# The last expert fold placed inside the preceding down product, and the slot sums turned by halves

## What is computed

```python
combine = jnp.sum(jax.nn.one_hot(global_idx, N_EXPERTS) * weights[..., None], axis=1)
y = jnp.zeros_like(x2d)
for e in range(N_EXPERTS):                       # 32 experts, each token chooses 2
    h = jax.nn.silu(x2d @ w_gate[e]) * (x2d @ w_up[e])
    y = y + combine[:, e:e + 1] * (h @ w_down[e])
```

## Time and profile before

| | |
|---|---|
| median of 3 runs | 1796.92 us |
| profiled execution: its own time | 1800.9 us |
| its span, first to last instruction | 1799.1 us |
| mean granted TensorE clock | 0.993 |
| PE busy | 1763.1 us (98%) |
| PE weight loads | 1528.9 us (85%) |
| DVE busy | 1157.0 us (64%) |
| ACT busy | 927.2 us (52%) |
| weights read | 317.74 MB, 177 GB/s over the span |

### The profile page before, as it was taken

The page is one execution under the profiler, slowest core; times in us unless marked ns, Lnnn a source line. Parts: engine busy times, 40 slices in busy tenths (PEclk is TensorE's granted clock), DMA queues, the critical chain, the costliest instruction groups (busy, mean ns, idle before and its releaser), DMA issues.

```text
span 1799.1 us, 25837 instructions
## 1 busy us (share of the span) xinstructions
PE 1763.1 (98%) x10654; PEld 1528.9 (85%) x10654; DVE 1157.0 (64%) x1452; ACT 927.2 (52%) x1239; POOL 116.7 (6%) x82
## 2 busy tenths in 40 slices
PE   7999999999999999999999999999999999999999
PEld 6999888899998888888898888888888988988887
DVE  5955577677775765468968655455545897765553
ACT  6444364466664644366754544354444666455442
POOL 1423011000000000000210000000000013000000
PEclk9999999999998999999999999999999999999999
DMA  8420135599997355545224555556554632346552
GB/s 275 133 74 1 43 111 213 189 391 387 383 386 274 117 187 187 184 146 185 71 95 141 179 183 184 183 183 187 187 187 152 199 118 71 118 142 208 183 181 106
DMA packets 179862, 320.47 MB, mean 178 GB/s; under 512 B 6560, under 2 KB 149280, under 8 KB 168096
## 3 DMA queue, kind: packets, MB, share of 16 engines
q1 hardware_dynamic: 179600, 318.29, 52.0%
q0 software_dynamic: 144, 0.52, 0.1%
HBM read 317.74 MB, written 1.05 MB: 177 GB/s over the span
## 4 chain that ended last, share of the span: by engine, by line
PE 87%; DVE 8%; ACT 3%; DMA 1%; issue 1%; POOL 0%; SPq 0%; DVEq 0%
PE ps L557 83%; PE ps L560 4%; DVE ring_lo L1592 2%; DVE arena L1581 2%; ACT arena L2454 1%; ACT rhi L2454 1%; DMA ring<-in_w_in 1%; ACT L2454 0%; DVE xnl L1581 0%; DVE small L2240 0%; DVE arena L2392 0%; DVE arena L1584 0%; POOL arena L3052 0%; DVE arena L2342 0%; DVE arena L1791 0%
## 5 line engine op out<-in xcount | busy, mean ns | idle before, releaser
L1592 DVE TENSOR_TENSOR ring_lo<-ring,rhi 128x2048 fp32r<-128x2048 f32 x266 | 608.7, 2290 | 267.0 <-ACT rhi L2454 266.6
L2454 ACT ACTIVATE rhi<-ring 128x2048 fp32r<-128x2048 f32 x266 | 503.7, 1904 | 145.3 <-PE ps L557 125.2
L557 PE MATMUL ps<-rhi,xnh 128*128 128x512 f32 (+2 forms) x784 | 307.9, 393 | 0.0
L557 PE MATMUL ps<-ring_lo,xnh 128*128 128x512 f32 (+2 forms) x800 | 307.4, 384 | 0.0
L557 PE MATMUL ps<-rhi,xnl 128*128 128x512 f32 (+2 forms) x784 | 302.2, 385 | 0.0
L557 PE MATMUL ps<-xnh,rhi 128*128 128x256 f32 (+1 forms) x760 | 221.3, 291 | 4.1 <-DVE xnl L1581 3.2
L2454 ACT ACTIVATE arena<-ps 128x512 f32<-128x512 f32 (+4 forms) x194 | 97.1, 518 | 244.9 <-PE ps L557 165.5
L557 PE MATMUL ps<-xnl,rhi 128*128 128x256 f32 (+1 forms) x760 | 215.9, 284 | 0.0
L557 PE MATMUL ps<-xnh,ring_lo 128*128 128x256 f32 (+1 forms) x760 | 215.8, 284 | 0.0
L557 PE MATMUL ps<-rhi,hhi 128*128 128x512 f32 x544 | 207.1, 397 | 0.0
L557 PE MATMUL ps<-arena 128*128 128x64 f32 (+11 forms) x1446 | 171.0, 291 | 6.1 <-DVE arena L2362 3.7
(11 more groups left out here) (249 smaller groups left out, 2131.5 us busy)
## 6 DMA issues: line engine op xcount, KB each, us to landing
ring<-in_few_gu SPq DMA_DIRECT2D x60, 1024.0 KB, 7.3
ring<-in_w_in SPq DMA_DIRECT2D x45, 1024.0 KB, 5.4
ring<-in_ffn_w_gate SPq DMA_DIRECT2D x88, 512.0 KB, 4.0
ring<-in_ffn_w_up SPq DMA_DIRECT2D x88, 512.0 KB, 5.0
ring<-in_ffn_w_down SPq DMA_DIRECT2D x44, 1024.0 KB, 4.9
ring<-in_exp_w_down SPq DMA_DIRECT2D x32, 1024.0 KB, 7.4
ring<-in_w_out SPq DMA_DIRECT2D x20, 1024.0 KB, 4.9
ring<-in_w_in SPq DMA_DIRECT2D x4, 896.0 KB, 4.7
```

Source lines behind the costliest of these rows:

```text
L557: return e.matmul(o, lhsT, rhs, start=start, stop=stop, skip_group_check=True)
L1592: e.tensor_tensor(lo, raw, f32(hi), SUB).then_inc(*w.hit("lo", n))
L2454: return e.activation(o, x, func, **kw)
```

## The change

Five things change.

1. SBUF layout: comb shrinks from 64 to 8 words, expert_of moves up behind it (56 words), first_slot becomes 48 words and stands last. Every later tile lies 128 bytes lower.
2. PE: for the last block the order becomes product(32, 0), turn(31), product(32, 1), first half of down(31), turn(32), second half of down(31), down(32). down(32) writes its halves to two banks (4 and 5) and signals each.
3. DVE: `few_place(31)` stands behind `few_gated(32)`; `few_place(32)` is two copies of half the size, each with its own wait and signal.
4. ACT: the split of the first `ffn(0)` tile stands behind `few_hidden(32)` instead of ahead of it.
5. `slot_sums`: PE turns the first halves of slots 0, 1 and 2 once the first half of the last copy is there, then the second halves; slot turn 2 uses banks 6 and 7. Spreads follow in another order. Work counts stay the same.

```diff
-        comb_ = sb("comb", 64)
+        comb_ = sb("comb", 8)
+        expert_of = sb("expert_of", 56, I32)
...
-        first_slot = sb("first_slot", NK, I32)
-        expert_of = sb("expert_of", 40, I32)
+        first_slot = sb("first_slot", 48, I32)
...
+        y_bank = [0, 2, 6, 0]
...
-            def few_down(j):
+            def few_down(j, halves=(0, 1)):
...
+                for half in halves:
+                    if BLOCKS[j][2]:
+                        b = 4 + 2 * (j % 2) + (half if j == NK - 1 else 0)
+                        if j == NK - 1:
+                            bank(b, ("few_y", j, half))
+                        elif not half:
+                            bank(b, ("few_y", j, 1))
+                        for dc in range(4 * half, 4 * half + 4):
...
+                    if half or j == NK - 1 or not BLOCKS[j][2]:
                         p.then_inc(*w.hit("few_down", j, half))
...
-                w.wait_ge("few_y", NK - 1, 1)
-                turn(0)
-                turn(1)
-                sum_banks("moe")
+                for half in range(2):
+                    w.wait_ge("few_y", NK - 1, half)
+                    for j in range(3):
+                        turn(j, half)
                 spread(0, 0)
-                turn(2)
+                turn(3, 0)
+                turn(3, 1)
+                spread(1, 0)
+                spread(2, 0)
                 spread(0, 1)
-                spread(1, 0)
-                turn(3)
-                spread(2, 0)
+                spread(3, 0)
                 spread(1, 1)
-                spread(3, 0)
                 spread(2, 1)
                 tile_turn(2, 0)
                 spread(3, 1)
...
+                    if j == NK - 1:
+                        few_down(j - 1, (0,))
+                        few_turn(j)
+                        few_down(j - 1, (1,))
+                        few_down(j)
+                    elif j:
                         few_down(j - 1)
...
+                    for half in range(2):
+                        w.wait_ge("few_down", j, half)
+                        e.tensor_copy(ys[:, 4 * half:4 * half + 4, at], src[half][:, 4 * half:4 * half + 4]).then_inc(*w.hit("few_y", j, half))
...
-                    if j >= 2:
+                    if 2 <= j < NK:
                         few_place(j - 2)
                     if j and BLOCKS[j - 1][2]:
                         few_gated(j - 1)
+                    if j == NK:
+                        few_place(NK - 2)
...
-                    if j == NK:
-                        part(ld(("ffn", 0, 0)))
                     if j:
                         few_hidden(j - 1)
```

More of the change, by code:

```diff
@@ L1104, in few_down @@
                 w.wait_ge("few_m" if BLOCKS[j][2] else "few_h", j)
[L1105 to L1113, removed]
+                for half in halves:
[6 more added lines that the diff above has]
+                        for dc in range(4 * half, 4 * half + 4):
+                            for k in range(2):
+                                p = mm(PS[b][:, 64 * dc:64 * dc + 64], wt[:, k, 128 * dc:128 * dc + 128], few_h[j % 2][:, k, 0:64], k == 0, k == 1)
+                    else:
                         b = 4 + 2 * (j % 2) + half
@@ L1119, in few_down @@
                                 p = mm(PS[b][:, 128 * q:128 * q + 128], wt[:, k, 128 * dc:128 * dc + 128], few_h[j % 2][:, k], k == 0, k == 1)
+                    if half or j == NK - 1 or not BLOCKS[j][2]:
                         p.then_inc(*w.hit("few_down", j, half))
-                if last_of(j):
+                if last_of(j) and 1 in halves:
                     spent[n] = ("few_down", j, 1)
@@ L1173, in slot_sums, with turn @@
             def slot_sums():
[L1174 to L1180, removed]
+                def turn(j, half):
+                    b = y_bank[j] + half
+                    bank(b, ("y_lo", j, half))
+                    for q in range(4):
+                        p = tr(PS[b][:, 128 * q:128 * q + 128], ys[:, 4 * half + q, 128 * j:128 * j + 128])
+                    p.then_inc(*w.hit("y_T", j, half))
                 def spread(j, tt):
@@ L1184, in spread @@
                     for dh in range(2):
+                        if not j:
+                            bank(sum_bank("moe", 2 * tt + dh), ("sum", "moe", 2 * tt + dh))
                         d = slice(512 * dh, 512 * dh + 512)
@@ L1234, in experts @@
                     down(ld(("moe_down", x)), 0, 2, hhi, hlo, "moe_down", x, k_of=lambda k: 2 * (x % 2) + k)
[L1235 to L1238, removed]
+                for j in range(NK):
+                    w.wait_ge("xw", j)
+                    few_product(j, 0)
                     if j:
                         few_turn(j - 1)
-                    if j < NK:
-                        few_product(j, 1)
+                    few_product(j, 1)
                     if j == 2:
                         slots_turned()
-                    if j:
+                    if j == NK - 1:
[4 more added lines that the diff above has]
+                    elif j:
                         few_down(j - 1)
@@ L1982, in starts @@
                 ts(first_slot[0:1, 1:2 * WIDE:2], start[:, 0:WIDE], 128.0, 512.0, ADD, ALU.min)
-                e.tensor_copy(first_slot[0:1, 2 * WIDE:], start[:, WIDE:]).then_inc(*w.hit("first_slot"))
+                e.tensor_copy(first_slot[0:1, 2 * WIDE:NK], start[:, WIDE:]).then_inc(*w.hit("first_slot"))
                 w.wait_ge("first_slot")
@@ L2032, in few_place @@
                 if BLOCKS[j][2]:
-                    w.wait_ge("few_down", j, 1)
-                    e.tensor_copy(ys[:, :, at], PS[4 + 2 * (j % 2)][:, :].rearrange("p (c n) -> p c n", c=8)).then_inc(*w.hit("few_y", j, 1))
+                    b = 4 + 2 * (j % 2)
+                    src = [PS[b + i][:, :].rearrange("p (c n) -> p c n", c=8) for i in range(2)]
+                    if j < NK - 1:
+                        w.wait_ge("few_down", j, 1)
+                        e.tensor_copy(ys[:, :, at], src[0]).then_inc(*w.hit("few_y", j, 1))
+                        return
+                    for half in range(2):
+                        w.wait_ge("few_down", j, half)
+                        e.tensor_copy(ys[:, 4 * half:4 * half + 4, at], src[half][:, 4 * half:4 * half + 4]).then_inc(*w.hit("few_y", j, half))
                     return
@@ L2102, in experts @@
                         w.wait_ge("slot_w")
-                        stt(yrl[:, j, d], PS[2 * (j % 2) + half][:, :], slot_w[:, j:j + 1], f32(yrh[:, j, d]), MUL, SUB).then_inc(*w.hit("y_lo", j, half))
+                        stt(yrl[:, j, d], PS[y_bank[j] + half][:, :], slot_w[:, j:j + 1], f32(yrh[:, j, d]), MUL, SUB).then_inc(*w.hit("y_lo", j, half))
                 part(ld(("ffn", 0, 0), 1))
@@ L2806, in experts @@
                         w.wait_ge("slot_w")
-                        act(yrh[:, j, d], PS[2 * (j % 2) + half][:, :], ACT.Copy, scale=slot_w[:, j:j + 1]).then_inc(*w.hit("y_hi", j, half))
+                        act(yrh[:, j, d], PS[y_bank[j] + half][:, :], ACT.Copy, scale=slot_w[:, j:j + 1]).then_inc(*w.hit("y_hi", j, half))
                 sqrt_table()
```

## The result

The changed kernel takes 1784.19 us (median of 4 runs, 1783.12 to 1785.71) against 1796.99 us before: ratio 0.993, 95% interval 0.9912 to 0.9947. The profiled execution shows even more: 1783.62 us with a span of 1781.8 us, against 1800.9 and 1799.1 before.

The account below looks back on a forecast made before the run. PE was taken as the bound, busy 98% of the span; gains of 1.04 + 3.54 + 0.65 + 3.08, layout zero, gave 8.3 us, 1792.6 us profiled, scaled to a median of 1788.6 us. Range: 1786.8 to 1794.0 us.

Parts of the forecast that it names:

- The stage: PE from the start of down(31) to the tile turn opening ffn(0): 18.9 us forecast against 27.23 before, gain 8.3 us.
- the 1.04 forecast: Folding turn(32) inside down(31) removes PE's wait, so down(32) starts at 570.05 instead of 571.09: gain 1.04 us.
- steps 2 and 3: Down(32) at full clock, 3.52 us not 7.06, gain 3.54; last copy in halves, idle 0.3 not 0.95, gain 0.65.
- The idle of 0.3 us: PE's remaining wait ahead of the first transpose, with DVE in its split until 573.3; 0.95 us before.
- The new idle ahead of the first spread: PE waits about 0.9 us before spread(0, 0), which needs y_lo of both halves of slot turn 0.
- 10.73: Slot sums, first transpose to tile turn: 10.73 us forecast against 13.81 before, gain 3.08 us.
- The extra copy: Halving the last copy costs DVE 0.15 us more, forecast as covered by PE's work.
- The clock step: Without the gap, down(32) runs at 2.4 GHz in 3.52 us instead of 7.06: gain 3.54 us.
- The rule that the prediction weighed: Transposes do not count as PE activity, so 2.5 us of them plus 0.9 us idle would read as one pause.
- Step 5: SBUF layout: no instruction added, no row showing an effect of 128 bytes of address, so zero gain taken.
- D: Rival, chance 0.04: 1446 + 544 matmuls reading lowered tiles lose 7 ns each to clashes; net 5.6 us slower, 1802.5 us.
- rival A: Chance 0.24: one slow stretch of 3.4 us, among the spreads or in the mixer, loses 1.7 us; gain 6.6, 1790.3 us.

Follow-up runs that it names:

- after_again: The changed kernel run once more, unaltered, beside later runs of the kernel before: 1783.06 us, ratio 0.991.
- order_only: The changed kernel with the five small tiles as before, so later tiles are back at their old addresses: 1791.95 us, ratio 0.9968.
- old_sums: The changed kernel with the slot sums in the old order, all behind the second half of the last copy: 1786.65 us.
- the four padded ones: The changed kernel with all tiles 128 bytes higher (1781.9 us), rhi and later tiles 128 higher (1794.41), rhi and constants 128 higher (1787.8), rhi and later 256 higher (1782.64).
- no_nest: The changed kernel with one PE edit undone, down(31) whole, then turn(32), then down(32): 1787.73 us.
- layout_only: The kernel before with comb of 32 words instead of 64, so all tiles behind it lie 128 bytes lower: 1792.5 us, ratio 0.9969.
- layout_plus128: The kernel before with comb of 96 words instead of 64, so tiles from rope on lie 128 bytes higher: 1792.45 us.
- distance_32: The kernel before with comb of 40 words instead of 64; arena, hhi and hlo 96 bytes lower, 32 bytes beyond the fast place: 1798.22 us.
- distance_64: The kernel before with comb of 48 words instead of 64; arena, hhi and hlo 64 bytes lower, 64 bytes beyond the fast place: 1798.62 us.

## Why the prediction was wrong

**The stage was right.** By its steps: down(32) started 4.46 us behind down(31)'s start (3.52 + 0.85 = 4.37 forecast), so 0.95 us of the 1.04 forecast came. down(32) to the first transpose took 3.64 us against 8.01 before; forecast were 3.82 us, the sum of steps 2 and 3. The idle of 0.3 us that was forecast ahead of the transposes did not come, since DVE was through with its split earlier. The new idle ahead of the first spread came as named, released by DVE's remainder, 0.69 us instead of 0.9. From first transpose to tile turn 10.90 us against 10.73. Together 8.23 us of a forecast 8.3. The extra copy and the moved splits cost nothing, as said: DVE's split ran from 570.45 to 572.73, and the first half copy was done at 573.07.

**The clock step was right for the changed kernel.** Every profiled execution with the nested order (after, after_again, order_only, old_sums and the four padded ones) ran the stage at full clock. The rule that the prediction weighed, from the Trainium skill, "TensorE: Matmul & The Clock Gate", section "Part 4: PE-mode transpose", would have the 24 transposes and the idle behind them count as one pause, 3.5 us long in the trace; the clock is 1.00 from 573.12 to 584.02, so no fall came of it here, nor in the seven other profiled executions with this order of the slot sums. The prediction's other premise, that the clock fell before because of the gap, is only in part borne out: with the gap back, the one profiled execution (no_nest) held the clock.

**Step 5 failed: the layout was taken at zero.** The prediction's words were that the rows give no reason for a gain. The runs show 18 ns in three matmuls, 8.4 us from the tile turn to the end in the profiled pair, and 6.1 (layout alone) to 10.05 us (layout on top of the order) in the medians. This alone takes the time below the range. The prediction had the mechanism among its rivals, D, but with one sign only: a clash of moved with unmoved tiles that would come. It did not ask whether such a clash was there already. The rows to ask stood in the trace of before, same shape and same moving tile: with ring_lo 389 ns for xnh but 395 and 394 for hhi and hlo, with rhi 390 for xnl but 395 for hlo. (The pair rhi with xnh and rhi with hhi is 397 both times and shows nothing; its starts do, 227 against 232 ns.) A difference between two groups that should be alike may be a price that is being paid, and here an edit that shifted addresses gave it back. Of D's two groups only the one with hhi gained (397 to 392); the 1446 matmuls of `ps<-arena` went from 291 to 290 ns.

**The step from the profiled execution to the median was off the other way.** The prediction scaled 1800.9 to 1796.92, which leaves the 8.3 us as they are. But part of the 4 us between the two lies in the stage itself. The profiled execution's slow stretch at the last down lasted 13.7 us, against 10.2 us in layout_only, layout_plus128, distance_32 and distance_64 (stage 25.7 us, not 27.23), and it had another near 172 that these lack. If the median execution has the shorter stretch, 25.7 - 19.0 = 6.7 us of the 8.2 reach it. This is an estimate: order_only's 6.65 us agree with it, but stand beside runs of before with a median of 1798.6; beside 1796.99 they would be 5.0. So the stage was likely overrated in the median while the layout was left out, and the two errors partly cancel.

**What rival A names does happen, but not by the change.** A slow stretch in the mixer (844 in layout_only, 838 in no_nest) costs the 1.7 us that were worked out for it: the rest is 1199.5 with it and 1197.5 to 1197.8 without. layout_only has the old order, and the kernel before had such a stretch near 172 itself, so they come with either order. The profile of the changed kernel has none there, that of after_again has one in the second layer's mixer (clock 0.57 over 1434 to 1438), at 1784.65 us. Such stretches are a likely cause of the 2.6 us over which the runs of the changed kernel spread; only two of them were profiled.

## What to carry to other kernels

Before an edit that moves tiles, compare groups of the same shape that differ only in a tile, from start to start; where they differ, work out the tiles' distances modulo 256 bytes (the step that fits the distances tried here), and count a possible gain as well as a loss. Where the clock was low behind a gap of PE, removing the gap may be worth more than its length; count that worth by how often the clock falls, not by one profiled execution, and look for slow stretches in that execution before its time is scaled to the median. Compare parts of a change beside the same runs of the kernel before; here its median moved by 3.2 us from one occasion to the next.

## What the hardware showed beyond what was expected

In this kernel matmuls of 512 columns in fp32r take 227 or 232 ns from start to start (medians), by the distance of the stationary tile to the ring that holds the moving weights: the two distances that are 0 modulo 256 bytes are fast; 32, 64 and 128 bytes off all cost the same. The matmul's own moving operand isn't the whole of it, since with rhi in line and the ring out of line both kinds are slow (236 and 234 ns). The Trainium skill, "TensorE: Matmul & The Clock Gate", section "Step-by-step: what each phase is for", says that loading the next tile's weights doesn't steal SBUF read bandwidth from the running matmul; no run here tests the two reads apart, and what the traces show is that 5 ns of 232 hang on where the tiles lie.

Behind one and the same gap of 0.78 us the clock fell in five profiled executions (before, layout_only, layout_plus128, distance_32, distance_64) and held in one (no_nest). Whether that is chance or something in which no_nest differs is open, since each of these kernels was profiled once.
